# Shift and scale of the first norm as columns on the turned rows, in both layers

## The reference

```python
mod   = jax.nn.silu(c)     @ ada_w[l] + ada_b[l]      # 6 x 1024 numbers for the tokens
mod_c = jax.nn.silu(c_ctx) @ ada_w[l] + ada_b[l]      # 6 x 1024 numbers for the context
sh1, sc1, g1, sh2, sc2, g2 = jnp.split(mod[:, None, :], N_MOD, axis=-1)
h  = modulate(rmsnorm(x,   norm_mix_g[l]), sh1,  sc1)   # rmsnorm(x, g) * (1 + scale) + shift
hc = modulate(rmsnorm(ctx, norm_mix_g[l]), csh1, csc1)
... # the mixer, the second norm, the experts; then at the end of the even layer:
x   = x   + g2  * f[:B * S].reshape(B, S, D)            # f: two expert rows per token, weighed and added
ctx = ctx + cg2 * f[B * S:].reshape(B, Lc, D)
```

## Time and profile before

| | us |
|---|---|
| median of three runs | 2298.84 |
| the profiled execution | 2299.72 |
| its span in the profile | 2297.9 |
| TensorE busy | 1970.1 (86%) |
| start of the first product of the even layer (L563) | 60.57 |
| end of the last expert product of the even layer, start of the odd layer's first product (L1609) | 843.5, 908.72 |

### The profile page before, as it was taken

How to read it: one execution, slowest core, us unless ns; L and a number is a source line. 1 busy time by engine, 2 the same in 40 slices (tenths; PEclk the granted TensorE clock), 3 DMA queues, 4 the chain that set the end, 5 groups by cost and what they waited for, 6 DMA issues and landing times.

```text
span 2297.9 us, 28359 instructions
## 1 busy us (share of the span) xinstructions
PE 1970.1 (86%) x12062; PEld 1112.9 (48%) x12062; DVE 606.9 (26%) x1313; ACT 368.4 (16%) x787; POOL 356.9 (16%) x280
## 2 busy tenths in 40 slices
PE   4999969988898754999969888888849989998898
PEld 4567444434443224445634333333317767765775
DVE  2144341111111114212532111111125132035852
ACT  2133220000000002012321000000011130041131
POOL 0024330000000102012521000000012042040120
PEclk8999979999999986999979999999978999999899
DMA  9348139999999966322747999999964423417221
GB/s 368 108 161 298 73 111 415 426 424 424 425 426 425 426 263 226 91 83 91 277 151 292 425 425 421 425 423 421 424 252 149 155 76 127 162 48 214 74 85 55
DMA packets 139084, 594.36 MB, mean 259 GB/s; under 512 B 19332, under 2 KB 30612, under 8 KB 105024
## 3 DMA queue, kind: packets, MB, share of 16 engines
q1 hardware_dynamic: 113168, 557.86, 61.0%
q10 hardware_dynamic: 19600, 28.07, 3.6%
q0 software_dynamic: 6176, 6.42, 0.8%
HBM read 582.71 MB, written 21.65 MB: 263 GB/s over the span
## 4 chain that ended last, share of the span: by engine, by line
PE 80%; issue 8%; DVE 5%; ACT 3%; POOL 2%; DMA 2%; POOLq 0%; SPq 0%; ACTq 0%; DVEq 0%
PE banks L1215 20%; PE banks L1240 10%; PE banks L2026 7%; PE banks L1192 5%; PE banks L1609 4%; PE banks L2028 4%; PE banks L946 4%; PE banks L563 3%; PE banks L1611 2%; PE banks L2226 2%; PE banks L2423 2%; PE banks L324 2%; PE banks L694 2%; PE banks L722 2%; PE banks L341 1%
## 5 line engine op out<-in xcount | busy, mean ns | idle before, releaser
L1215 PE MATMUL banks<-RG,HT 128*64 128x512 f32 x2112 | 481.5, 609 | 89.0 <-issue 87.5
L1215 PEld LDWEIGHTS banks<-RG,HT 128*64 128x64 f32 x2112 | 172.4, 140 | 385.9 <-issue 383.7
L1344 POOL DMA_INDIRECT y_rows<-AR x66 | 64.4, 976 | 905.4 <-DVE AR L1244 892.4
L1224 DVE TENSOR_TENSOR AR<-AR,banks 128x256 f32<-128x256 f32 x66 | 39.7, 602 | 555.6 <-ACT AR L1220 496.7
L2026 PE MATMUL banks<-HT,RG 128*128 128x256 f32 x768 | 170.1, 383 | 0.7 <-ACT HT L443 0.7
L2026 PEld LDWEIGHTS banks<-HT,RG 128*128 128x128 f32 x768 | 146.9, 192 | 23.4 <-issue 2.4
L1192 PE MATMUL banks<-AR 128*128 128x256 bf16 x1152 | 149.9, 279 | 3.4 <-DVE AR L1181 3.4
L1220 ACT ACTIVATE AR<-banks 128x256 f32<-128x256 f32 x66 | 25.3, 383 | 786.6 <-PE banks L1215 786.6
L1192 PEld LDWEIGHTS banks<-AR 128*128 128x128 bf16 x1152 | 110.2, 100 | 62.9 <-issue 49.0
L1240 PE MATMUL banks<-RG,AR 128*64 128x512 f32 x528 | 120.6, 598 | 2.6 <-DVE AR L1233 2.6
L1240 PE MATMUL banks<-AR 128*64 128x512 f32 x528 | 120.6, 598 | 2.6 <-DVE AR L1233 2.6
(11 more groups left out here) (365 smaller groups left out, 2325.0 us busy)
## 6 DMA issues: line engine op xcount, KB each, us to landing
RG<-in_moe_w SPq DMA_DIRECT2D x165, 2048.0 KB, 19.9
AR<-in_moe_w SPq DMA_DIRECT2D x33, 2048.0 KB, 21.9
RG<-in_ada_w SPq DMA_DIRECT2D x24, 2048.0 KB, 8.5
RG<-in_attn_w_in SPq DMA_DIRECT2D x20, 2048.0 KB, 7.8
RG<-in_odd_w_in SPq DMA_DIRECT2D x6, 2048.0 KB, 16.8
RG<-in_ssm_w_in SPq DMA_DIRECT2D x4, 2048.0 KB, 9.5
AR<-y_rows ACTq DMA_DIRECT2D x6, 1024.0 KB, 8.8
RG<-in_even_w_in SPq DMA_DIRECT2D x2, 2048.0 KB, 20.2
```

Of the source, the lines that this page charges most:

```text
L1215: m = pe.matmul(p[64 * h:64 * h + 64, :], x[:, k, :], w[:, :, k, 256 * h:256 * h + 256], start=k == 0, stop=k == 7)
L1344: g.indirect_dma_start(y, off, E.Y[b], None, bounds_check=2047, oob_is_err=False).then_inc(*event)
```

## The change

`rstd` commutes with turning as a factor of a row, and the other three numbers are, once the rows are turned, one number per partition. The new kernel uses this.

- Each part of the ada rows, with its bias, is turned once by one 128-column transpose (`pe_ada_cols`), and eight numbers per partition are taken from it (`dve_ada_cols`). The result is `COLS[l]`: for each half of 512 columns and each stream four columns of 128 numbers. The gains of both layers are loaded as 16 rows of 128 and turned once (`GC`). For these parts the spreads of both layers, their 16 copies and the tiles `M1` go.
- Layer 0: the tiles of x are loaded ahead of the bias, the eight `even_loads` are issued after the root instead of before it. The tiles are only multiplied with `rstd` (one `tensor_scalar` each) and turned while the pieces of `ada_w` arrive. When the columns are there, VectorE modulates the 256 token columns of `HT` in place, ScalarE the 256 context columns, 8 instructions of 128x256 each.
- Layer 1: the columns are made in the even attention, where the rows were made. At the boundary the four tiles are joined, normed and turned one behind the other. ScalarE weighs the first expert row and multiplies with rstd, VectorE does the rest of the join, `XS` included. When a tile is copied out of PSUM it is modulated: the first half by ScalarE (4 instructions of 128x128), the second by VectorE (4 as well). GpSimd has no part in either norm or in this join (`dve_combine` and `pool_combine` are no longer called here). The 512 KB gain load goes.

The core of the diff, of which small renamings are left out:

```diff
-        M1 = {(0, 0): ar(KK, D), (1, 0): ar(0, D), (0, 1): ar(3 * KK, D), (1, 1): ar(2 * KK, D)}
+
+        SVF = SVT[:].rearrange("p a b -> p (a b)")
+        COLS = [SVF[:, 544 + 32 * l:576 + 32 * l].rearrange("p (a s k) -> p a s k", a=2, s=2) for l in range(2)]
+        GC, GR = SVF[:, 608:624], ar(10 * KK, 128)
...
+        def pe_ada_cols(pe, l, n, raw, bank, before):
+            pe.wait_ge(*at("ada_raw", l, n))
+            if before is not None:
+                pe.wait_ge(*at(*before))
+            pe.transpose(PS[bank][:, 0:128], raw, IDN[:]).then_inc(*ev("ada_turned", l, n))
+
+        def dve_ada_cols(v, l, n, bank):
+            o = COLS[l][:, n // 2, :, 4 * (n % 2):4 * (n % 2) + 4]
+            t = PS[bank][:, 0:128].rearrange("p (j s) -> p s j", j=4)[:, 0:2, :]
+            v.wait_ge(*at("ada_turned", l, n))
+            if n < 2:
+                ins = v.tensor_copy(o, t)
+            else:
+                g = bc(GC[:, 8 * l + 4 * (n % 2):8 * l + 4 * (n % 2) + 4], 1, 2)
+                ins = v.scalar_tensor_tensor(out=o, in0=t, scalar=1.0, in1=g, op0=ADD, op1=MUL)
+            ins.then_inc(*ev("ada_cols", l, n))
...
+            act.wait_ge(*at("x_loads", 3))
+            act_squares(act, "mix0", range(4), ar(9 * KK, D))
+            act_root(act, "mix0", n=4)
             for i, (o, s) in enumerate((
...
-            run(act_ada(act, 0, ada_first(), M1))
-            act.wait_ge(*at("x_loads", 3))
-            act_squares(act, "mix0", range(4), ar(9 * KK, D))
-            act_root(act, "mix0", n=4)
-            act_first_norm(act, "mix0")
+            for t in range(4):
+                act_turn(act, "mix0", t)
+            act.wait_ge(*at("turned_out", "mix0", 3, 1))
+            for hf in range(2):
+                act.wait_ge(*at("ada_cols", 0, 2 + hf))
+                for k in range(4 * hf, 4 * hf + 4):
+                    h = HT[:, k, 256:512]
+                    ins = act.activation(h, h, ACT.Identity, scale=COLS[0][:, 1, 1, k:k + 1], bias=COLS[0][:, 0, 1, k:k + 1])
+                ins.then_inc(*ev("modulated_ctx", hf))
...
-            run(pe_ada(pe, 0, ada_first()))
-            pe.wait_ge(*at("ada_scale", 0, 3, 1))
-            pe_first_norm(pe, "mix0")
+            for n in range(4):
+                pe_ada_rows(pe, 0, n, n % 2, ("ada_raw", 0, n - 2) if n >= 2 else None)
+                if n == 0:
+                    pe.wait_ge(*at("ab_loads", 1))
+                    pe.transpose(PS[3][:, 0:16], GR[0:16], IDN[0:16, 0:16]).then_inc(*ev("gain_turned"))
+                pe_turn(pe, "mix0", n, XN[n], ("normed", "mix0", n), ("mix0", n - 2) if n >= 2 else None)
+                pe_ada_cols(pe, 0, n, MB[:, n % 2, :], 2 + n % 2, (None, ("gain_cols",), ("ada_cols", 0, 0), ("ada_cols", 0, 1))[n])
...
+            dve_rstd(v, "mix0", D, n=4)
+            for t in range(4):
+                v.tensor_scalar(XN[t], XS[:, t, :], ST[:, 16 + t:17 + t], None, MUL).then_inc(*ev("normed", "mix0", t))
             v.wait_ge(*at("ab_loads", 1))
-            run(dve_ada(v, 0, ada_first(), M1, GB))
-            v.wait_ge(*at("ada_plain", 0, 1, 1))
-            v.wait_ge(*at("ada_scale", 0, 3, 1))
-            v.wait_ge(*at("x_loads", 3))
-            dve_first_norm(v, "mix0")
+            v.wait_ge(*at("gain_turned"))
+            v.tensor_copy(GC, PS[3][:, 0:16]).then_inc(*ev("gain_cols"))
+            v.wait_ge(*at("gain_cols"))
+            for n in range(4):
+                dve_ada_rows(v, 0, n, n % 2, MB[:, n % 2, :], AB, ("ada_turned", 0, n - 2) if n >= 2 else None)
+                dve_ada_cols(v, 0, n, 2 + n % 2)
+            v.wait_ge(*at("turned_out", "mix0", 1, 1))
+            for hf in range(2):
+                v.wait_ge(*at("ada_cols", 0, 2 + hf))
+                for k in range(4 * hf, 4 * hf + 4):
+                    h = HT[:, k, 0:256]
+                    ins = v.tensor_scalar(h, h, COLS[0][:, 1, 0, k:k + 1], COLS[0][:, 0, 0, k:k + 1], MUL, ADD)
+                ins.then_inc(*ev("modulated", hf))
...
+                        if ci == 0 and t % 2 == 0 and k % 4 == 0:
+                            pe.wait_ge(*at("modulated_ctx" if t else "modulated", k // 4))
...
-                pe_ada_rows(pe, 1, n, 7, ("ada_raw", 1, n - 1) if n else spread_out(0, 11, 1))
+                pe_ada_rows(pe, 1, n, 7, ("ada_cols", 1, n - 1) if n else spread_out(0, 11, 1))
+                yield
+                pe_ada_cols(pe, 1, n, MB[:, n % 2, :], 7, None)
                 yield
...
-                dve_ada_rows(v, 1, n, 7, ROWS[:, n, :], AB1, None)
+                dve_ada_rows(v, 1, n, 7, MB[:, n % 2, :], AB1, ("ada_turned", 1, n - 2) if n >= 2 else ("ada_spread", 0, 10 + n, 1))
+                yield
+                dve_ada_cols(v, 1, n, 7)
...
-            act.wait_ge(*at("h_out", 0, 31))
-            act.dma_start(GB, rows(I["norm_mix_g"][1])).then_inc(*dm("gain1_load"))
...
-            for x, (n, s) in enumerate(SPREADS):
-                pe_ada_spread(pe, 1, n, s, ROWS[:, n, :], 2 + x % 4, spread_out(1, *SPREADS[x - 4]) if x >= 4 else None)
-            pe.wait_ge(*at("ada_scale", 1, 3, 1))
-            pe_first_norm(pe, "mix1")
+            for t in range(4):
+                pe_turn(pe, "mix1", t, NW[t % 2], ("row_scaled", t), ("mix1", t - 2) if t >= 2 else None)
...
-                act_ada_spread(act, 1, n, s, M1[(n // 2, s)], 2 + x % 4)
-            act.wait_ge(*at("combined", 0, 3))
-            act_squares(act, "mix1", range(4), ar(17 * KK + 512, D))
-            act_root(act, "mix1", n=4)
-            act_first_norm(act, "mix1")
+            act_join(act, 0)
+            for i in range(6):
+                if i + 1 < 4:
+                    act_join(act, i + 1)
+                if i < 4:
+                    act.wait_ge(*at("joined_rows", i))
+                    act.activation(E0.Z[i][:, 0, :], XS[:, i, :], ACT.Square,
+                                   accum_out=ST[:, i:i + 1]).then_inc(*ev("squares", ("mix1", i)))
+                if 1 <= i <= 4:
+                    t = i - 1
+                    act_root(act, ("mix1", t), at_=t)
+                    if t >= 2:
+                        act.wait_ge(*at("turned", "mix1", t - 2, 1))
+                    act.wait_ge(*at("rstd", ("mix1", t)))
+                    act.activation(NW[t % 2], XS[:, t, :], ACT.Copy, scale=ST[:, 16 + t:17 + t]).then_inc(*ev("row_scaled", t))
+                if i >= 2:
+                    t = i - 2
+                    act.wait_ge(*at("turned", "mix1", t, 0))
+                    for k in range(4):
+                        ins = act.activation(HT[:, k, 128 * t:128 * t + 128], PS[4 + 2 * (t % 2)][:, 128 * k:128 * k + 128],
+                                             ACT.Identity, scale=COLS[1][:, 1, t // 2, k:k + 1],
+                                             bias=COLS[1][:, 0, t // 2, k:k + 1])
+                    ins.then_inc(*ev("turned_out", "mix1", t, 0))
+
+        def act_join(act, t):
+            z = E0.Z[t][:, 0, :]
+            act.wait_ge(*at(f"z_load{t}", 0))
+            act.activation(z, z, ACT.Copy, scale=E0.WT[:, t, 0:1]).then_inc(*ev("first_weighed", t))
 
         def dve_odd_begin(v):
-            v.wait_ge(*at("gain1_load"))
-            for x, (n, s) in enumerate(SPREADS):
-                dve_ada_spread(v, 1, n, s, M1[(n // 2, s)], GB, 2 + x % 4)
-            v.wait_ge(*at("ada_plain", 1, 1, 1))
-            v.wait_ge(*at("ada_scale", 1, 3, 1))
-            dve_first_norm(v, "mix1")
-
-        def pool_odd_begin(g):
-            g.wait_ge(*at("ada_plain", 1, 1, 1))
-            pool_first_norm(g, "mix1")
+            for i in range(6):
+                if i < 4:
+                    z, gate = E0.Z[i], mods0[(5, i // 2)]
+                    v.wait_ge(*at("first_weighed", i))
+                    vstep(v, v.scalar_tensor_tensor(out=z[:, 1, :], in0=z[:, 1, :], scalar=E0.WT[:, i, 1:2], in1=z[:, 0, :],
+                                                    op0=MUL, op1=ADD))
+                    vstep(v, v.tensor_tensor(z[:, 1, :], z[:, 1, :], gate, MUL))
+                    v.tensor_tensor(XS[:, i, :], XS[:, i, :], z[:, 1, :], ADD).then_inc(*ev("joined_rows", i))
+                if 1 <= i <= 4:
+                    dve_rstd(v, ("mix1", i - 1), D, at_=i - 1)
+                if i >= 2:
+                    t = i - 2
+                    v.wait_ge(*at("turned", "mix1", t, 1))
+                    for k in range(4, 8):
+                        ins = v.tensor_scalar(HT[:, k, 128 * t:128 * t + 128],
+                                              PS[5 + 2 * (t % 2)][:, 128 * (k - 4):128 * (k - 4) + 128],
+                                              COLS[1][:, 1, t // 2, k:k + 1], COLS[1][:, 0, t // 2, k:k + 1], MUL, ADD)
+                    ins.then_inc(*ev("turned_dve", "mix1", t, 1))
```

64 lines of the change are left out of this document (20 added, 44 removed).

## The result

The changed kernel took **2263.51 us** (median of 4 runs, 2262.89 to 2263.87) against 2298.95 for the kernel before (2298.69 to 2301.65, 4 runs on the same chip): **ratio 0.9843, 95% interval 0.9826 to 0.986**. I had forecast 2267, with 2259 to 2277. The profiled execution took 2263.87, its span is 2262.0 (before: 2299.72 and 2297.9).

What follows compares the result with a forecast made beforehand. TensorE's chain bounds nearly everywhere, broken at both first norms. 2299.72 - 15.5 (head) + .8 (attention) - 17.0 (boundary) = 2268.0 for the profiled execution, so 2267 median; own range 2262 to 2273, 8 in 10 for 2259 to 2277.

Steps and rivals of the forecast that it cites:

- head 15.5: Layer 0's first norm: even product starts at 45.0 instead of 60.57 us, gain 15.5, bounds 12.5 to 18.
- boundary 17.0: Last expert product to first odd product: odd product starts at 891.7 instead of 908.72, gain 17.0, bounds 14 to 20.
- attention +.8: Even attention: one product of the rows per stage, with transposes and exchange with VectorE, costs .8 us, bounds -1 to 4.
- the two breaks: TensorE's chain of waits breaks at both first norms: head, product at 60.78 us, and boundary of the layers, 65 us.
- what is won comes through: After each break, weight fetches wait for products, not wall-clock time, so gains of 15.5 and 17.0 us come through whole.
- one gain is given back: Experts' stretch: transfers tied to something earlier turn the head's 15.5 us into waits for weights; 2283, 6 in 100.
- 512 KB are 1.3 us: the piece lands at 38.5: Head: without the 512 KB gain transfer, the fourth `ada_w` piece lands 1.3 us earlier, at 38.5 instead of 39.8.
- the second rival: Head: ScalarE is held up by issuing its own `even_loads`, losing 3 to 5 us; 2271, 8 in 100.
- The narrow forms: Boundary: narrow modulating instructions take .3 us each on VectorE and .4 on ScalarE.
- 32.4 us of them 'issue', in which TensorE has nothing to do: Boundary of the layers: 32.4 of the 65 us before the odd product are TensorE idle without work.
- Clock: Even and odd products: rival that TensorE's low clock lasts into them, with fewer matmuls before; 2331, 3 in 100.

Runs made afterwards that it cites:

- Head alone: Only layer 0's first norm changed, boundary of the layers as before, against the kernel before: 2277.80 us, ratio .9911.
- nested: TensorE's skipped overflow blocks put one inside the other, in the kernel before (2292.53 us) and in the changed kernel (2260.53 us).
- padded: 40 unread 32x32 transposes added at TensorE's start, in the kernel before (2289.94 us, ratio .9960) and in the changed kernel (2268.66 us, .9868).

## Why the prediction was right, and what in it was wrong

The time was right: 2267 forecast, 2263.5 measured, inside the narrower range of 2262 to 2273. The sum came out 4.1 above the profiled execution (2268.0 against 2263.87), and its terms have these errors: head 15.5 for 14.17, boundary 17.0 for 15.73, attention +.8 for -2.2 (with the experts), and 4.2 in a last part that I had at nothing. The near hit is in part luck: the 4.2 are no work of the change, and neither are 3 to 6 of the boundary's 15.7.

- **Right: the two breaks, and that what is won comes through.** Head alone keeps its 14.4 but for 1.1 up to the last part (+.6 to the last expert, +.5 to the states); the experts' stretch, from the first product behind the attention (L946 at 231.38, L972 at 214.91) to the last expert product, is 612.10 before and 612.18 after. The rival "one gain is given back" is refuted.
- **Head, right in its chain, off in sizes.** Fourth piece at 39.75, not 38.5: the step "512 KB are 1.3 us: the piece lands at 38.5" failed. From there 6.6 us against 6.5, by errors that cancel: the product took 3.64 (I took 2.48, from a row with the granted clock at .75; here TensorE had waited 5.64 us, and over the product it was .50), the turn 1.28 instead of 1.97. VectorE's modulating is .335 for .35, ScalarE's 4.04 for 4. The issues of `even_loads` took .35 to .53 each and held nobody: the second rival is refuted too.
- **Attention: wrong in sign.** A product of the rows takes 1.95 to 1.96, and a stage with one, its transpose included, 2.0 more than one without: the exchange with VectorE is wholly covered. My 2.45 for a product came from the one stage with the stop of .78. Of the -2.2, 1.1 are the even product (68.98 for 70.10 from its start at 60.57; granted clock 1.00 over its first 10 us, for .88) and 1.2 the attention behind it, .8 of them that stop. So the step "cost .8" failed: the change costs the attention nothing that can be seen, and what was won there isn't its work either.
- **Boundary: near in its sum, wrong in what sets it.** The first rows were there 11.2 us after the last expert product instead of 13.3, since the gain load in front of them had cost 3 us and not 1.3. From there to the product it is 38.3 us where I had 34.9; nested it is 33.6. The narrow forms were at .34 to .38 for .3 and .4. What I had missed is the step before: "32.4 us of them 'issue', in which TensorE has nothing to do". It did: with the walk gone the boundary is 44.9 after and 57.5 before. And of the 15.7 only 10 to 13 are the change's: compare kernels with the same walk, 59.4 and 60.4 against 47.4 to 49.5 at five packets, 65.2 against 52.6 and 53.2 at six, 57.5 and 44.9 nested.
- **Clock.** The granted clock was .50 from 865 to 875, .75 over the next 10 us and 1.00 from 885. It rose within the first product, as before; that rival is refuted.

How large is the change's gain, then? As the kernels stand 35.4 us. Nested 32.0 (2292.53 to 2260.53), padded 21 (ratios .9960 and .9868). The sign is safe, the size is not a property of the change alone.

## What to carry to other kernels

An idle engine whose releaser is "issue" may not be free: look at what stands in its program there, and at the instruction packets of that window. Rows of skipped conditional blocks are worth trying one inside the other; here that took 4.6 and 7.8 us off a boundary. Where a change gains in stretches that it doesn't touch, build the kernel with some instructions more at an idle place before the gain is put down to the change. When a wait for a transfer remains, ask what is issued while that transfer flies: moving 1.57 MB that nobody needed yet was worth 5 us, with no change to any instruction's work.

## What I had not expected of the hardware

- Jumping over 14 blocks of TensorE costs 22 to 28 us (30 to 36 of idle time less the 8.4 that are left with one jump over all); on ScalarE, with few instructions in a block, the same 14 seem to cost 1.8 us.
- Code of the same work is up to 10 us faster or 5 us slower by 40 instructions ahead of it (2300.3 to 2289.9; 2263.5 to 2268.7).
- 512 KB ahead of the expert rows delay them by 3.0 us, and 1.57 MB beside a 2 MB piece in flight delay it by 5.0 to 6.1. At the 5.3 us for 2 MB that two landings in the head show, their shares are 1.3 and 4.1.
- A narrow VectorE instruction with two columns costs .335 at 128x256 from SBUF and .34 at 128x128 from PSUM (1.36 / 4). One with one column costs .685 at 128x1024 from SBUF (2.74 / 4): a quarter of the width still takes half the time.
